# Delta rule heads: query transposes, output transposes and output gate moved behind three block joins, decay exponentials apart, first GpSimd mask tied to the lane inverse

## The reference, cut to what matters

```
q, k, v = silu(causal_conv(h @ w_in))          # per head, 128 wide
q, k = l2_norm(q) * 128**-0.5, l2_norm(k)
decay[i,j] = exp(gc[i] - gc[j]) for i >= j     # gc: running sum of the gate g
a = strict_lower((k*beta) @ k.T * decay)
u, w = solve(I + a, [v*beta, k*beta*exp(gc)])  # unit lower triangular
qk = lower(q @ k.T * decay)
for each chunk:                                # state S, one chunk after another
    v_new = u - w @ S
    o     = (q*exp(gc)) @ S + qk @ v_new
    S     = S*exp(gc_end) + (k*exp(gc_end - gc)).T @ v_new
o = rms_norm(o, gain) * silu(z)                # then @ w_out
```

## Time and profile before

| | |
|---|---|
| Runs, median of 3 | 3050.88 us (3050.23 to 3052.8) |
| The profiled execution | 3050.12 us, its span 3048.4 us |
| TensorE busy over the span | 2762.6 us, 91% |
| VectorE, ScalarE, GpSimd busy | 51%, 28%, 26% |
| Delta rule: first fill to last output turn | about 46 to 817 us of the span |
| Head 4, from the start of its scan (436.2) to that of head 5 (527.9) | 91.7 us; TensorE busy 81.8, VectorE 48.5, ScalarE 38.5, GpSimd 28.8 us; mean granted clock 0.94 |
| Heads 1, 2, 3, 5 and 6, the same way | 91.7, 90.5, 90.7, 89.1, 91.0 us |

### The profile page before, as it was taken

How to read it: one execution, slowest core, us unless ns; L and a number is a source line. 1 busy time by engine, 2 the same in 40 slices (tenths; PEclk the granted TensorE clock), 3 DMA queues, 4 the chain that set the end, 5 groups by cost and what they waited for, 6 DMA issues and landing times. The chain is left out here.

```text
span 3048.4 us, 35919 instructions
## 1 busy us (share of the span) xinstructions
PE 2762.6 (91%) x13277; PEld 2296.6 (75%) x13277; DVE 1563.2 (51%) x1780; ACT 866.6 (28%) x1213; POOL 779.0 (26%) x372
## 2 busy tenths in 40 slices
PE   7789898888597999999998599999688999999996
PEld 5677777777576888888887487788576888888885
DVE  4455545555234454544455675567354454444555
ACT  5244444344332111111111334333332111111112
POOL 2333223332142222222222211111232222222223
PEclk8799999999798999999999799999898999999998
DMA  2010110010242111111111310110332111111112
GB/s 106 21 42 28 34 41 34 28 41 7 71 151 83 49 48 48 48 41 55 48 48 48 119 35 31 46 48 34 130 119 77 49 41 48 55 48 48 48 62 97
DMA packets 62892, 172.11 MB, mean 56 GB/s; under 512 B 6177, under 2 KB 23137, under 8 KB 62833
## 3 DMA queue, kind: packets, MB, share of 16 engines
q1 hardware_dynamic: 62832, 171.33, 16.5%
HBM read 146.11 MB, written 25.20 MB: 56 GB/s over the span
## 5 line engine op out<-in xcount | busy, mean ns | idle before, releaser
L151 POOL TENSOR_TENSOR f_wlo<-f_raw,f_whi 128x1024 fp32r<-128x1024 f32 x132 | 335.6, 2551 | 1082.8 <-ACT f_whi L171 1082.8
L61 PE MATMUL f_up<-x_hi,f_whi 128*128 128x512 f32 x1408 | 550.4, 391 | 23.0 <-POOL f_wlo L151 23.0
L62 PE MATMUL f_up<-x_lo,f_whi 128*128 128x512 f32 x1408 | 549.7, 390 | 0.0
L63 PE MATMUL f_up<-x_hi,f_wlo 128*128 128x512 f32 x1408 | 549.6, 390 | 0.0
L171 ACT ACTIVATE f_whi<-f_raw 128x1024 fp32r<-128x1024 f32 x132 | 139.8, 1059 | 935.5 <-PE f_up L63 505.9
L61 PEld LDWEIGHTS f_up<-x_hi,f_whi 128*128 128x128 f32 x1408 | 265.6, 189 | 79.1 <-POOL f_wlo L151 23.8
L62 PEld LDWEIGHTS f_up<-x_lo,f_whi 128*128 128x128 f32 x1408 | 265.7, 189 | 55.3
L63 PEld LDWEIGHTS f_up<-x_hi,f_wlo 128*128 128x128 f32 x1408 | 265.4, 189 | 55.5
L61 PE MATMUL f_down<-f_whi,f_hhi 128*128 128x512 f32 x704 | 277.2, 394 | 17.5 <-issue 16.0
L211 DVE TENSOR_TENSOR acc<-f_down,acc 128x512 f32<-128x512 f32 x320 | 217.1, 689 | 123.2 <-PE f_down L63 120.3
L62 PE MATMUL f_down<-f_wlo,f_hhi 128*128 128x512 f32 x704 | 276.3, 392 | 0.0
(11 more groups left out here) (356 smaller groups left out, 4809.6 us busy)
## 6 DMA issues: line engine op xcount, KB each, us to landing
f_raw<-in_ffn_w_up SPq DMA_DIRECT2D x88, 512.0 KB, 3.2
f_raw<-in_ffn_w_down SPq DMA_DIRECT2D x44, 512.0 KB, 3.2
g_raw<-in_gdn_w_in SPq DMA_DIRECT2D x32, 512.0 KB, 3.5
l_raw<-in_gla_w_in SPq DMA_DIRECT2D x26, 512.0 KB, 3.3
after_ffn_xt<-x_mid SPq DMA_DIRECT2D x16, 512.0 KB, 4.1
first_xt<-in_x SPq DMA_DIRECT2D x8, 512.0 KB, 8.1
g_columns<-cum_rows SPq DMA_DIRECT2D x8, 512.0 KB, 3.8
mixed<-g_zc SPq DMA_DIRECT2D x8, 512.0 KB, 2.9
```

Source lines behind the costliest of these rows:

```text
L61: pe.matmul(out, w_hi, x_hi, start=first, stop=False)
L62: pe.matmul(out, w_hi, x_lo, start=False, stop=False)
L63: return pe.matmul(out, w_lo, x_hi, start=False, stop=last)
L151: pool.tensor_tensor(w_lo[k][:, :], raw[k][:, :], w_hi[k][:, :].bitcast(F32), ALU.subtract) \
```

## The change

Seven edits, all in the delta rule:

1. TensorE, `prepare`: `output_turn(h - 1)` stands behind `joined(h, 2)`; before, it stood behind fill 18, ahead of the second join. The wait for the gate (`s_og`) moves along. `queries_by_token(h)` leaves the end of the scan and stands behind fill 24. The fills between the joins move by one.
2. TensorE: the wait for the query squares moves from the first join to `query_key_products`; `coupled(h, 0)` waits for the coupling matrix instead.
3. VectorE, `scan`: `near_back` directly behind `near_joined(h, True)`, at chunk 4; `conv_q(h, (1,))` goes from chunk 4 to chunk 5.
4. VectorE, `prepare`: the query factors are those of head h-1, at the start; `output_sums` and `output_norm` of head h-1 together behind join 0; two taps of `conv_v` ahead of join 1 and one behind; the decayed queries behind that; `output_gate`, the query sums and the next head's decay exponent (`start_head`, `head_decay`) behind join 2, ahead of the product that makes `attn`.
5. The exponentials: `from_start_exp(h + 1)` and `decay_exp(h + 1)` are two functions, each with its own semaphore, and run before the values are scaled and after. The exponent is made in place in `columns` once the first exponential has read it.
6. ScalarE: `silu(qT)` leaves the scan (chunk 6) for `prepare`, between `output_squares` and the second `m1_copies`; `evict(h, 1, 1)` and `high(h, 3)` move from the end of the scan to behind the first `m1_copies`; the last z eviction of a head moves into the next scan, behind chunk 0's copy. `output_deviation` stands behind `m1_copies(h, 1)`.
7. GpSimd: `coupling(h, 0)` waits for the new semaphore `near_blocks_inverted`, raised by the last instruction of `near_joined(h, True)`, and stands ahead of the two spreads; in head 0 `split(h, 2)` goes ahead of it.

The output's squares use `wTn` instead of `inv` as their buffer. No instruction's shape changes. The core of the diff:

```diff
@@ -1041,10 +1042,14 @@
                 near_blocks(h)
+                if peeled(h):
+                    split(h, 2)
+                pool.wait_ge(s_inverted, h + 1)
+                coupling(h, 0)
                 spread(h, 0)
                 spread(h, 1)
-                coupling(h, 0)
-                split(h, 2)
+                if not peeled(h):
+                    split(h, 2)
                 if not final(h):
...
@@ -1091,13 +1096,17 @@
-            def decay_exps(h):
-                act.wait_ge(s_dm, h + 1)
-                act.activation(decay[:, :, :], decay[:, :, :], ACT.Exp).then_inc(s_dx, 1)
+            def from_start_exp(h):
                 act.wait_ge(s_col, 16 * h + 16)
...
                     act.wait_ge(s_qd, h)
-                act.activation(from_start[:, :, :], by_chunk(columns), ACT.Exp).then_inc(s_dx, 1)
+                act.activation(from_start[:, :, :], by_chunk(columns), ACT.Exp).then_inc(s_fsx, 1)
+
+            def decay_exp(h):
+                if not peeled(h):
+                    act.wait_ge(s_ap, h)
+                act.wait_ge(s_dm, h + 1)
+                act.activation(decay[:, :, :], by_chunk(columns), ACT.Exp).then_inc(s_dx, 1)
...
@@ -1118,20 +1127,23 @@
                               3: lambda: (evict(h, 0, 1), high(h, 2)),
-                              5: lambda: evict(h, 1, 0),
-                              6: lambda: silu(qT, 3 * h + 2)}
+                              5: lambda: evict(h, 1, 0)}
                 for n in range(NT):
...
                         act.activation(vn[n % 2][:, :], pt[:, T:T + P], ACT.Copy).then_inc(s_vn, 1)
+                    if n == 0 and projects and not peeled(h):
+                        evict(h - 1, 3, 1)
                     if n in beside:
                         beside[n]()
-                if projects:
-                    act.wait_ge(s_qtok, h + 1)
-                    act.activation(wTn[:, :, :], by_chunk(pm), ACT.Square).then_inc(s_qsq, 1)
-                    evict(h, 1, 1)
-                    if not final(h):
-                        high(h, 3)
+
+            def query_squares(h):
+                act.wait_ge(s_qtok, h + 1)
+                act.activation(wTn[:, :, :], by_chunk(pm), ACT.Square).then_inc(s_qsq, 1)
+
+            def query_deviation(h):
+                act.wait_ge(s_qss, h + 1)
+                act.activation(stdq[:, :], ssq[:, :], ACT.Sqrt, bias=eps[:, 0:1]).then_inc(s_qstd, 1)
...
@@ -1171,32 +1183,46 @@
                     output_copy(h - 1)
-                m1_copies(h, 0)
+                if peeled(h):
+                    evict(h, 1, 1)
+                    m1_copies(h, 0)
+                else:
+                    m1_copies(h, 0)
+                    evict(h, 1, 1)
+                if not final(h):
+                    high(h, 3)
                 if not peeled(h):
                     output_squares(h - 1)
-                act.wait_ge(s_qss, h + 1)
-                act.activation(stdq[:, :], ssq[:, :], ACT.Sqrt, bias=eps[:, 0:1]).then_inc(s_qstd, 1)
+                silu(qT, 3 * h + 2)
+                m1_copies(h, 1)
                 if not peeled(h):
...
                     output_norm(h - 1)
-                evict(h, 2, 0)
-                m1_copies(h, 1)
+                if not final(h):
+                    evict(h, 2, 0)
+                m1_copies(h, 2)
                 silu(vT, 3 * h + 3)
-                m1_copies(h, 2)
-                evict(h, 2, 1)
+                if not final(h):
+                    evict(h, 2, 1)
                 if not final(h):
                     high(h, 4)
+                query_squares(h)
+                if not final(h):
+                    from_start_exp(h + 1)
                 scale_values(h)
+                if final(h):
+                    evict(h, 2, 0)
+                    evict(h, 2, 1)
                 if not final(h):
+                    decay_exp(h + 1)
                     evict(h, 3, 0)
...
                     key_squares(h + 1)
-                    decay_exps(h + 1)
                     key_deviation(h + 1)
-                    evict(h, 3, 1)
+                query_deviation(h)
...
@@ -1276,23 +1303,21 @@
+            def key_chain(h):
+                mask_decay(h)
+                key_sums(h)
+                key_factors(h)
+
...
                 dve.drain()
-                dve.wait_ge(s_col, 16 * h + 16)
-                dve.tensor_tensor(decay[:, :, :], by_chunk(columns), wide(hg[:, G_CUM, :]), ALU.subtract)
-                dve.drain()
-                dve.tensor_scalar(decay[:, :, :], decay[:, :, :], 0.0, None, ALU.min).then_inc(s_dm, 1)
-
-            def key_chain(h):
-                start_head(h)
-                head_decay(h)
-                key_sums(h)
-                mask_decay(h)
-                key_factors(h)
+                dve.wait_ge(s_fsx, h + 1)
+                dve.tensor_tensor(by_chunk(columns), by_chunk(columns), wide(hg[:, G_CUM, :]), ALU.subtract)
+                dve.drain()
+                dve.tensor_scalar(columns[:, :], columns[:, :], 0.0, None, ALU.min).then_inc(s_dm, 1)
             def mask_decay(h):
-                dve.wait_ge(s_dx, 2 * h + 1)
+                dve.wait_ge(s_dx, h + 1)
                 dve.tensor_tensor(decay[:, :, :], decay[:, :, :], each(upper[:, :]), ALU.mult)
...
@@ -1372,7 +1397,8 @@
                     dve.drain()
-                    dve.tensor_reduce(out=x[:, n:B, 0:n], in_=product, axis=AX_X, op=ALU.add, negate=True)
+                    dve.tensor_reduce(out=x[:, n:B, 0:n], in_=product, axis=AX_X, op=ALU.add, negate=True) \
+                        .then_inc(s_inverted, 1)
...
@@ -1395,13 +1421,12 @@
                               3: lambda: (near_rows(h, (7,)), near_joined(h, False)),
-                              4: lambda: (near_joined(h, True), conv_q(h, (1,))),
-                              5: lambda: near_back(h),
+                              4: lambda: (near_joined(h, True), near_back(h)),
+                              5: lambda: conv_q(h, (1,)),
                               6: lambda: conv_q(h, (2, 3))}
...
                         beside[0] = lambda: (coupling_matrix(h), conv_q(h, (1, 2, 3)))
-                        beside[4] = lambda: near_joined(h, True)
-                        del beside[6]
+                        del beside[5], beside[6]
                 for n in range(NT):
...
@@ -1443,26 +1468,37 @@
-            def prepare(h):
+            def query_sums(h):
                 dve.wait_ge(s_qsq, h + 1)
...
+
+            def query_factors(h):
+                dve.wait_ge(s_qstd, h + 1)
+                dve.reciprocal(rq[:, :], stdq[:, :])
+                dve.drain()
+                dve.tensor_scalar(rq[:, :], rq[:, :], float(P) ** -0.5, None, ALU.mult)
+                dve.drain()
+
+            def prepare(h):
+                if not peeled(h):
+                    query_factors(h - 1)
+                join(h, 0)
                 if not peeled(h):
                     output_sums(h - 1)
+                    output_norm(h - 1)
+                conv_v(h, (1, 2))
+                join(h, 1)
+                conv_v(h, (3,))
+                dve.wait_ge(s_silu, 3 * h + 2)
                 dve.tensor_tensor(qdT[:, :, :], by_chunk(qT), from_start[:, :, :], ALU.mult).then_inc(s_qd, 1)
-                join(h, 0)
-                if not peeled(h):
-                    output_norm(h - 1)
-                conv_v(h, (1,))
+                dve.tensor_copy(chunk_decay[:, :], hg[:, G_CHUNK, :])
+                join(h, 2)
                 if not peeled(h):
                     output_gate(h - 1)
-                conv_v(h, (2, 3))
-                dve.wait_ge(s_qstd, h + 1)
-                dve.reciprocal(rq[:, :], stdq[:, :])
-                dve.drain()
-                dve.tensor_scalar(rq[:, :], rq[:, :], float(P) ** -0.5, None, ALU.mult)
-                dve.tensor_copy(chunk_decay[:, :], hg[:, G_CHUNK, :])
-                join(h, 1)
-                join(h, 2)
+                query_sums(h)
+                if not final(h):
+                    start_head(h + 1)
+                    head_decay(h + 1)
                 dve.wait_ge(s_g, h + 1)
...
@@ -1604,6 +1641,7 @@
             def query_key_products(h):
+                pe.wait_ge(s_qsq, h + 1)
                 for c in range(NT):
...
@@ -1664,35 +1702,37 @@
                 pe.wait_ge(s_first, 2 * h + 2)
-                pe.wait_ge(s_qsq, h + 1)
+                pe.wait_ge(s_at, h + 1)
                 coupled(h, 0)
...
                 some(17, 18)
+                coupled(h, 1)
+                some(19)
+                joined(h, 1)
+                some(20, 21)
+                coupled(h, 2)
+                some(22)
+                joined(h, 2)
                 if not peeled(h):
                     output_turn(h - 1)
-                some(19)
+                some(23)
+                fill(h, 24)
                 if not peeled(h):
                     pe.wait_ge(s_og, h)
-                coupled(h, 1)
```

(62 more changed lines are left out.)

## The result

| | before | after |
|---|---|---|
| Median of 12 runs each | 3050.76 us (3048.83 to 3052.80) | 3055.64 us (3049.63 to 3063.15) |
| Ratio, 95% interval | | 1.0017 [1.0009, 1.0025] |
| Span of the profiled execution | 3048.4 us | 3052.5 us |
| Scan of head 1 starts (first value product) | 163.3 | 148.9 |
| Scan of head 7 starts | 709.3 | 712.7 |

From differences of these rows: head 0 won 14.4 us, the loop of six heads lost 17.8, head 7 won 2.8, and the tail lost 2.1 up to its output turn and 1.4 from there to the end. That is the 4.1 us between the spans.

The account below looks back on a forecast made before the run. TensorE, busy 91% of the span, was taken as the bound. A loop head gets 15.1 added less 13.9 removed, +1.2; six heads +7, head 0 -11: -4, so 3047 us. Range 3019 to 3065, the forecast's own 3041 to 3053.

Parts of the forecast that it names:

- Where the waits would stand: TensorE, each loop head: new waits of 3.6 (chunk 5's state), 2.9 (join 1), 2.3 (decayed query-key product), 1.1 and 0.8.
- The key turn's 1.1: TensorE's key turn would wait 1.1 us for ScalarE's copy of w, ready at 46.7 where TensorE is at 45.6.
- The clock: Slow stretches on TensorE: 4.4 us a head removed, two added behind the 3.6 and 2.9 waits at 2.2 each, 4.4.
- a rival at 25%: Exponentials sit on the path: the 2.3 wait for the decayed product takes the clock down too; +12, 3059, 25%.
- the 2.27: A 2.27 us wait in the earlier trace, followed by a slow stretch: product at 787.91 took 2.92 instead of 1.95.
- The period's own bound, 94 us: A loop period under 89 us or over 94 would show the forecast wrong.
- Head 0: Fill 16's 12.83 us wait for a weight split goes; with the other terms -11 us, bounds -6 and -15.
- the companions: Head 0's other terms: keys +2, join 1 wait -5, spreads +2.8, mask 1 +2.4, later waits +3.1, slow stretches -3.5.
- Head 7 and the tail: Head 7 taken as 0 (-3 to +3); the tail as 0, its output chain being as long as before.
- The removed 9.5 us of waits: TensorE's delta-rule waits, 9.8 us a head, would go except 0.3 at chunk 4.
- The table load: ScalarE's table load taken as 1.28 us without extra drain; the rival that a switch costs more: +16, 3063, 3%.
- The lock: GpSimd's 2.38 us mask holds VectorE's turn-back scalings, giving the 3.6 wait; rival not held: 1.25, 3020, 10%.

Follow-up runs that it names:

- e2: The changed kernel with GpSimd's first mask product back behind both spreads, without the new wait: 3030.47 us, 0.9932 of the kernel before.
- e3: The changed kernel with VectorE's output_norm behind the two value taps instead of ahead of them: 3003.41 us, 0.9847 of the kernel before.
- e1: The changed kernel with ScalarE's from-start exponential ahead of the query squares, their sums behind the decayed query-key product: 3043.85 us, 0.9985 of the kernel before.
- e7: The changed kernel with one fill moved from behind the value turn to ahead of it: 3046.47 us, 0.9978 of the kernel before.
- e5: The kernel before with only head 0's second weight split on GpSimd moved ahead of the spreads and mask: 3040.05 us, 0.9960.
- e4: The changed kernel with three edits at once: mask product back behind spreads, output_norm behind two value taps, first exponential ahead of query squares: 2984.99 us, 0.9787 of the kernel before.

## Why the prediction was wrong

The forecast was -4, the result +5, the other way. By its own steps:

- *Where the waits would stand:* right, all three, and their sizes nearly: 3.11, 2.57 and 2.18 for 3.6, 2.9 and 2.3; 0.71 for 0.8. The chains behind them are shown by e2 (the mask holds the scalings), e3 (the output's factors) and e1 (the squares ahead of the exponential). The key turn's 1.1 is mostly not seen (1.0 in all): the slow fills behind the value turn cover it, and where these are gone (e7, e1) it is 1.3 and 1.6. Idle time a head: forecast +1.2, measured -0.3.
- *The clock: the step that failed.* "I charge two slow stretches, those behind 3.6 and 2.9, at the mean of the old two, 2.2: 4.4." That let the clock cancel, 4.4 removed and 4.4 added a head. Removed were 3.5 (21.1 us in six heads) and added 6.8 (40.5). Of the 14.1 us added beyond the charge, 9.1 are a stretch charged at nothing, the one behind 2.18, which stands in every head; 9.6 are the stretch behind the third product, 22.8 us or 3.8 a head where 2.2 was charged; and -4.6 the one behind 3.1, 8.6 or 1.4 a head. e7 and e1 show the first: without the 2.18 wait 12.6 us of slow clock go, 9.1 net in e7. The text had this one as a rival at 25% with +12 on the sum, from "the 2.27" of the earlier trace rows, and it is what came. The mis-sized stretch stood in no rival. The period's own bound, 94 us, was too wide to tell: the loop came to 93.96.
- *Head 0:* -14.4 for -11, within its bounds. The cause was named right (e5 alone gives -13.7); that -11 was near is partly luck, since the companions, which were to add and take several us each, come to 0.7 in all.
- *Head 7 and the tail:* 0 and 0 were taken; -2.8 and +2.1 came. What shortened head 7 was not tested. The tail's, for the most part, is ScalarE's root with its table load, which stands ahead of the first copy: TensorE waits 2.56 us for `g_vn` where it waited 0.95.

```profile
792.49 1.28 ACT L1146 ACT_TABLE_LOAD   x1
793.79 0.30 ACT L1146 ACTIVATE g_stdq<-g_ssq,eps 128x8 f32<-128x8 f32 x1
794.00 0.26 ACT L1134 ACTIVATE g_vn<-g_pt 128x128 f32<-128x128 f32 x1
```

- *The removed 9.5 us of waits:* right. *The table load:* right too: the root starts 0.02 us after it ends, so the extra drain that the Trainium skill names ("ScalarE: Activation LUTs", "What ACT_TABLE_LOAD costs") isn't seen here either. *The lock:* the Trainium skill's rule ("SBUF — State Buffer", "Who interferes with whom") agrees with the trace for the strided scalings as well, 2.96 beside the mask and 0.80 without it. That they run in the mode which the rule asks for is not shown by itself.

In numbers, forecast and measured: loop +7 and +17.8 (idle -1.6, clock +19.4), head 0 -11 and -14.4, head 7 0 and -2.8, tail and rest 0 and +3.5: -4 and +4.1.

What stays open is why the same wait drops the clock in one head and not in another. Behind 3.1 in the changed kernel it fell at 267.73 and stayed up at 456.85; behind 2.2 in e3 it did both. The runs show that with fewer long waits the others cost less (the third product's stretch falls from 22.8 to 15.3 in e2), not by what rule.

## What to carry to other kernels

Split a loop of TensorE into idle and busy time and compare both before costing a move: here 17.8 us were lost with no more idle time than before. Several short waits can cost less than one long one: cutting 2.2 us into 0.8, 1.0 and 1.3 won 9 us with more waiting in all. And try the named edit alone first: here output turn and gate were worth 34 us, and the companions that came with them hid that.

## What was unexpected of the hardware

- The clock's price is in part shared. Taking away one wait of 2.57 (e3) took away 14.6 us of idle time and 32.4 of slow clock, some 8 of it behind waits that stayed; no wait of 1.6 or less was followed by a slow stretch in any head of e4, while 2.2 was in six heads of six of the changed kernel and in four of e3.
- A product of 128x8 on VectorE took 1.78 us beside GpSimd's product of two whole tiles, and a tap 2.57 instead of 1.28. Where small instructions stand in a chain, what GpSimd does at that moment counts more than their size.
